# Attention of a two-layer trunk: value products of two pairs of heads in one visit, eight buffers of transposed probabilities

## The reference, cut to what matters

```
s = q_h @ k_h.T * 96 ** -0.5                # 256 x 256, causal
p = softmax(where(key_pos <= q_pos, s, -inf))
o_h = p @ v_h                               # 256 x 64
mix = concat(o_h) @ w_o                     # 1024 -> 1024
```

## Time and profile before

| | |
|---|---|
| time, median of 3 runs | 1316.43 us (1316.16 to 1317.01) |
| the profiled execution | 1316.43 us, of which the span on the core is 1314.7 us |
| PE busy | 1305.5 us, 99% of the span |
| DVE, ACT busy | 642.6 us, 283.1 us |
| head pipeline (PE's steps 5 to 20) | 59.39 to 89.05 us |
| rest of the output projection | to 109.1 us |
| dense layer, recurrent block | to 437 us |
| experts | to the end, at 399 GB/s |

### The profile page before, as it was taken

How to read it: one execution, slowest core, us unless ns; L and a number is a source line. 1 busy time by engine, 2 the same in 40 slices (tenths; PEclk the granted TensorE clock), 3 DMA queues, 4 the chain that set the end, 5 groups by cost and what they waited for, 6 DMA issues and landing times.

```text
span 1314.7 us, 25495 instructions
## 1 busy us (share of the span) xinstructions
PE 1305.5 (99%) x10916; PEld 767.0 (58%) x10916; DVE 642.6 (49%) x1458; ACT 283.1 (22%) x424; POOL 86.1 (7%) x112
## 2 busy tenths in 40 slices
PE   9999999999999999999999999999999999999998
PEld 5778888888896544444444444444444444444444
DVE  5978666666776253333532523323353353342436
ACT  4774333333584100010010010001001001000102
POOL 2401111111001100000000000000000000000100
PEclk9999999999999999999999999999999999999999
DMA  8724555556467899999999999999999999999992
GB/s 295 289 79 163 192 191 191 191 191 208 159 254 294 328 406 402 420 406 414 420 420 405 418 420 407 415 420 411 411 420 411 395 419 420 405 405 420 419 412 98
DMA packets 124264, 441.93 MB, mean 336 GB/s; under 512 B 7314, under 2 KB 17764, under 8 KB 109572
## 3 DMA queue, kind: packets, MB, share of 16 engines
q1 hardware_dynamic: 119536, 424.57, 82.0%
q0 software_dynamic: 4560, 15.85, 3.3%
q10 hardware_dynamic: 68, 0.02, 0.0%
HBM read 430.84 MB, written 9.57 MB: 335 GB/s over the span
## 4 chain that ended last, share of the span: by engine, by line
PE 95%; DVE 1%; ACT 1%; DMA 1%; issue 0%; SPq 0%; DVEq 0%
PE psum L1509 66%; PE psum L426 8%; PE psum L427 8%; PE psum L428 8%; PE psum L1482 1%; PE psum L1147 1%; DMA raw<-in_mla_w_in 1%; DVE w_lo L406 1%; PE psum L1515 0%; ACT res L883 0%; ACT gain_mla L792 0%; ACT early L792 0%; PE psum L1357 0%; PE psum L442 0%; PE psum L1264 0%
## 5 line engine op out<-in xcount | busy, mean ns | idle before, releaser
L1509 PE MATMUL psum<-raw_more,hT 128*32 128x512 f32 x1656 | 535.7, 592 | 0.0
L1509 PE MATMUL psum<-raw,hT 128*32 128x512 f32 x1032 | 334.8, 592 | 0.0
L1509 PE MATMUL psum<-raw_more,xg_odd 128*32 128x512 f32 x1680 | 245.4, 592 | 0.0
L1509 PE MATMUL psum<-raw_more,xg 128*32 128x512 f32 x1704 | 241.8, 592 | 0.8 <-DVE xg L2222 0.8
L1509 PEld LDWEIGHTS psum<-raw_more,hT 128*32 128x32 f32 x1656 | 146.9, 109 | 122.6 <-issue 122.6
L2258 DVE STREAM_TRANSPOSE hT<-hid 32x128 f32<-32x128 f32 x672 | 205.1, 305 | 10.3
L2248 DVE SCALAR_TENSOR_TENSOR hid<-hid,psum 96x512 f32<-96x512 f32 x55 | 37.6, 684 | 303.2 <-PE psum L1509 302.4
L1095 ACT ACTIVATE hid<-psum 96x1024 f32<-96x1024 f32 (+1 forms) x32 | 29.2, 913 | 664.8 <-PE psum L1509 475.7
L1509 PE MATMUL psum<-raw,xg_odd 128*32 128x512 f32 x1008 | 147.7, 592 | 0.0
L1509 PE MATMUL psum<-raw,xg 128*32 128x512 f32 x984 | 144.2, 592 | 0.0
L1509 PEld LDWEIGHTS psum<-raw,hT 128*32 128x32 f32 x1032 | 91.1, 109 | 76.0 <-issue 75.8
(11 more groups left out here) (316 smaller groups left out, 1341.7 us busy)
## 6 DMA issues: line engine op xcount, KB each, us to landing
raw_more<-in_moe_w_gate SPq DMA_DIRECT2D x71, 1024.0 KB, 17.2
raw_more<-in_moe_w_up SPq DMA_DIRECT2D x70, 1024.0 KB, 16.9
raw_more<-in_moe_w_down SPq DMA_DIRECT2D x69, 1024.0 KB, 17.1
raw<-in_moe_w_down SPq DMA_DIRECT2D x43, 1024.0 KB, 17.4
raw<-in_moe_w_up SPq DMA_DIRECT2D x42, 1024.0 KB, 16.7
raw<-in_moe_w_gate SPq DMA_DIRECT2D x41, 1024.0 KB, 17.5
raw<-in_ffn_w_gate SPq DMA_DIRECT2D x14, 1024.0 KB, 5.1
raw<-in_ffn_w_up SPq DMA_DIRECT2D x14, 1024.0 KB, 5.8
```

Source lines behind the costliest of these rows:

```text
L1509: return pe.matmul(psum[rows_q, bank, cols], stationary, moving, start=start, stop=stop, tile_position=(0, rows_q.start), skip_group_check ...
```

## The change: what it does

`values(0)` and `values(1)` go together into PE's step 8 (before: 6 and 8), `values(2)` and `values(3)` into step 12 (10 and 12), `values(4)` and `values(5)` into step 16 (14 and 16); `values(6)` and `values(7)` stay at 18 and 20. `o_high` and `o_low` of the eight pairs are at steps 9, 10, 13, 14, 17, 18, 19, 21 (before: 7, 9, 11, 13, 15, 17, 19, 21). `probs_T` has eight buffers, in the first two thirds of `early`, and `pT_copy(h)` waits for value products only from h = 8 on.

```diff
-        probs_T = early[:, 0, 0:12 * P].rearrange("p (b n) -> p b n", b=4)
+        probs_T = early[:, 0:2].rearrange("p a n -> p (a n)")[:, 0:24 * P].rearrange("p (b n) -> p b n", b=8)
+
+        VALUES_AT = {8: (0, 1), 12: (2, 3), 16: (4, 5), 18: (6,), 20: (7,)}
+        PARTS_AT = {9: 0, 10: 1, 13: 2, 14: 3, 17: 4, 18: 5, 19: 6, 21: 7}
...
             def pT_copy(h):
                 act.wait_ge(probsT_ps, h + 1)
-                if h >= 4:
-                    act.wait_ge(o_ps, (h - 4) // 2 + 1)
-                copy(probs_T[:, h % 4, :], psum[:, 4 + h % 2, 0:3 * P]).then_inc(probsT_ready, 1)
+                if h >= 8:
+                    act.wait_ge(o_ps, (h - 8) // 2 + 1)
+                copy(probs_T[:, h % 8, :], psum[:, 4 + h % 2, 0:3 * P]).then_inc(probsT_ready, 1)
...
# ACT's loop
-                if i >= 7 and i % 2 == 1:
-                    o_high((i - 7) // 2)
+                if i in PARTS_AT:
+                    o_high(PARTS_AT[i])
...
# values(g): probs_T[:, h % 4, ...] becomes probs_T[:, h % 8, ...] in both products
...
# PE's loop
-                if i >= 6 and i % 2 == 0:
-                    values((i - 6) // 2)
+                for g in VALUES_AT.get(i, ()):
+                    values(g)
...
# DVE's loop
-                if i >= 7 and i % 2 == 1:
-                    o_low((i - 7) // 2)
+                if i in PARTS_AT:
+                    o_low(PARTS_AT[i])
```

More of the change, by code:

```diff
@@ L1278, in values @@
                     c0 = h * V + half_v * 32
-                    pe.matmul(psum[rows_o, 6 + g % 2, 0:T], v[:, 0, c0:c0 + 32], probs_T[:, h % 4, 0:T],
+                    pe.matmul(psum[rows_o, 6 + g % 2, 0:T], v[:, 0, c0:c0 + 32], probs_T[:, h % 8, 0:T],
                               start=True, stop=False, tile_position=(0, rows_o.start))
@@ L1282, in values @@
                     c0 = h * V + half_v * 32
-                    mm = pe.matmul(psum[rows_o, 6 + g % 2, P:T], v[:, 1, c0:c0 + 32], probs_T[:, h % 4, T:3 * P],
+                    mm = pe.matmul(psum[rows_o, 6 + g % 2, P:T], v[:, 1, c0:c0 + 32], probs_T[:, h % 8, T:3 * P],
                                    start=False, stop=True, tile_position=(0, rows_o.start))
```

## The result

| | before | changed |
|---|---|---|
| median of 22 runs | 1316.45 us (1316.04 to 1317.39) | 1318.18 us (1317.82 to 1320.36) |
| ratio, 95% interval | | 1.0014 [1.0008, 1.0019] |
| span of the profiled run | 1314.7 us | 1317.7 us |
| start of `transpose_qk(6)`, where the two programs first differ | 61.10 us | 62.21 us |
| from the start of `transpose_qk(6)` to the start of `values(7)` | 27.16 us | 29.00 us |

The change costs 1.7 us of 1316, some 0.14%; the interval of the ratio leaves no change out. The two profiled spans differ by more, 3.00 us, and the table says where: 1.11 us ahead of the first step that differs, 1.84 in the head pipeline, 0.05 behind it. The first of these is not the change's.

What follows compares the result with a forecast made beforehand. PE and ACT were taken as both full in the head pipeline, with PE carrying its shift to the end. Terms 0.14 + 0.89 + 0.15 + 0.47 = +1.65 us on 1316.43 gave 1318.1 us; 8 in 10 range 1316.2 to 1319.2.

Steps and rivals of the forecast that it cites:

- The path to the end: Behind the head pipeline: whatever the pipeline gains or loses is carried unchanged to the end of the kernel.
- The switches saved: On PE in the head pipeline: five visits to the value products instead of eight save 3 x 0.28 = 0.84 us.
- What the lump does: Head pipeline: a 1.60 us block of values starves ACT, then PE waits for its copies; +0.14 steps 6-8, +0.89 steps 9-12.
- the replay: Queues of PE, ACT and DVE stepped by durations, order and dependence from PE's step 6: +1.65 us, varied +1.2 to +1.9.
- The stall given back: Steps 13 to 17: moving o_low(4) gains 0.8 at transpose_probs(13), used up by the starved group; +0.15 us more.
- The wait of `values(6)`: Step 18: values(6) needs bank 6 from o_high(4) and o_low(4), now in step 17; +0.47 us.
- Rival (1): Head pipeline: switches are the price, the block costs nothing; -0.84 or -1.6 us, 1314.8 to 1315.6; chance 0.10.
- Rival (2): Head pipeline: ACT bounds but waits for nothing, so no change, 1316.0 to 1316.9 us; chance 0.12.
- Rival (3): PE's some seven stalls cost 0.2 more each, or standing still lowers its clock; 1319.5 us; chance 0.08.

Runs made afterwards that it cites:

- the padded pair: Kernel before and changed kernel, each with ten more products with zeros ahead of each of scores(6) to scores(15): 1322.29 and 1321.84 us.
- part 4 moved: Changed kernel with the high and low part of pair 4 in step 16 instead of 17: 1317.73 us.
- the eight buffers alone: Changed kernel's eight buffers of transposed probabilities, with value products and their copies at the steps of before: 1316.65 us, ratio 1.0002.
- the blocks joined singly: Order of before with one block joined: only pairs 4 and 5 (parts of pair 4 in step 16), 1316.34 us; only pairs 2 and 3, 1317.95 us.

## Why the prediction was right, step by step

Forecast 1318.1 us (+1.65), measured 1318.18 (+1.73 in the medians, +1.84 by the meter). That the time agrees to 0.1 us is in part luck: by the meter the forecast was 0.19 low, nearly all of it in one term. The steps, as distances from `transpose_qk(6)` before and changed:

| step | before | changed | measured | predicted |
|---|---|---|---|---|
| to `transpose_qk(9)` | 6.36 | 6.46 | +0.10 | +0.14 |
| to `transpose_qk(13)` | 13.90 | 14.96 | +0.96 more | +0.89 |
| to `transpose_probs(13)` | 22.26 | 23.46 | +0.14 more | +0.15 |
| to `values(6)` | 24.46 | 26.28 | +0.62 more | +0.47 |
| to `values(7)` | 27.16 | 29.00 | +0.02 more | 0 |

- **The path to the end.** The stretch behind `values(7)` is the same to 0.05 us. That the last values carry everything behind them was right.
- **The switches saved.** Right in kind and size: 0.28 each taken, 0.55 for two measured with the padding, 0.33 for one added ahead of score products. The rows of before give only 0.25 for one (0.09 ahead, 0.13 and 0.03 behind); the prediction's 0.19 behind was rounded to fit the pair, and the padded pair bears the 0.28 out. The Trainium skill's rule in "TensorEngine Tiling (Array Packing)", Key Properties, that a change of mode drains the array, agrees with both. The runs here show the price of a switch, not that it is a drain; and the price did not decide.
- **What the lump does.** Right: ACT waits 0.37 and 0.39 behind a block (predicted 0.47 and 0.50), PE waits 0.33 and 0.24 for it two steps later (0.47 and 0.46). For ACT the difference is one of counting: a bracket runs from the end of the instruction before, which lies 0.10 behind the point at which the next could have started (0.58 and 0.48 for `qk_copy`), the replay from that point. For PE it is too: by the starts `scores(10)` comes 0.50 and `scores(11)` 0.40 later than the 0.22 behind the transposes of k that a step without a wait shows (71.78 to 72.50, 73.87 to 74.49). Ahead of the first block `scores(7)` came 0.20 late where the prediction had 0.31. The period of four heads is 8.50 instead of 8.45.
- **The stall given back.** The 0.76 ahead of `transpose_probs(13)` did vanish and was used up, as forecast: 0.68 of wait at `scores(15)` in its place.
- **The wait of `values(6)`.** Cause right, shown by part 4 moved: 0.61 off the meter. Size low by 0.15: `o_low(4)` started 2.24 behind `transpose_probs(13)` (85.67 to 87.91) where the replay had 2.18, and from its end at 88.33 to the values at 88.49 it is 0.16 where I took 0.05. I had counted 0.10 of restart for score products only.
- **Rival (1)**, only the switches count, fails where ACT is full and holds up to `transpose_qk(13)` where it is not: the padded pair is that rival, made true so far. Its whole 0.84 is not reached even there (0.49 at `values(7)`), for `values(6)` still waits for pair 4. **Rival (2)**, ACT without waits, fell by ACT's brackets. **Rival (3)**: PE had six stalls of the kind (five with a bracket, and `scores(7)`), the granted clock stayed at 1.00, and the whole loss was 0.19 above the replay, not 0.2 for each stall. The rival of the experiments, a price of the blocks or the buffers themselves, fell by the eight buffers alone (27.18), the padded pair, and the blocks joined singly: the last one costs nothing (26.97 with it and without it), the middle one 1.57.

## What to carry to other kernels

- Where two engines are both full over a period, a saving on one is worth at most the difference of their sums, here 0.04 us per pair of heads by the rows of before (3.77 against 3.73), and not its own 0.28. Sum the other engine's starts before counting a gain.
- Joining small pieces of work on a producer saves switches and makes a lump. What it costs depends on its place: here a single block costs nothing at the last pairs and 1.57 us in the middle. That the two buffers of transposed q and k are what keeps PE from running ahead is read from the waits in the code; no run here has deeper ones, so it is not shown. Test a lump by slowing the producer: if the sign turns, it is starvation, and the brackets say of whom.
- For effects of 0.1% compare a distance inside the trace from the first step that differs; the start of this kernel alone moved by more than 1 us between profiles.

## What the runs showed that the prediction did not have

- A single block in the middle cost 1.57 us and three cost 1.84 (foreseen only in the expectation of that run, from the traces so far); what made it dear was a wait of 0.85 on DVE two steps later, for a PSUM bank.
- PE's bracket at `values(6)` named the instruction that ended nearest, 0.04 us ahead of the start, and not the one it waited for, which had ended 0.16 ahead. Value products that waited for `o_low` in the single block also started 0.15 behind its end (79.61 to 79.76). Check a bracket against the waits in the code before blaming what it names.
- A switch that was added ahead of score products cost 0.33 us, one saved ahead of transposes 0.28: the return to score products costs more.
